# Projection, norm and turns chained per 128 tokens, layer parameters and sine tables loaded elsewhere

## The chip, the cores and the metric

One core of a Trainium2 chip runs the whole program; the metric is device time in microseconds (us) of one execution. TensorE (PE) multiplies and turns tiles, VectorE (DVE) and ScalarE (ACT) do the elementwise work, GpSimd (POOL) splits weights, and the queue of SyncE (SP) starts the weight DMAs.

## The reference

Four layers run over 512 tokens of width 1024, all in float32: two of a first kind (differential attention beside an mLSTM), two of a second kind (retention beside stick-breaking attention, then an MLP). What matters here is their frame:

```python
h = rmsnorm(x, g)            # x * rsqrt(mean(x*x) + eps) * g, per token
proj = h @ w_in              # then the branches, a gated merge u
x = x + u @ w_o              # the projection back
# second kind only:
h = rmsnorm(x, g_mlp); x = x + relu(h @ w_up)**2 @ w_down
# at the end
return rmsnorm(x, g_final)
```

The first kind also needs `cos` and `sin` of position times 32 frequencies. So there are seven norms: one of the input, five between a projection back and the next matrix product, and the last, whose result is the output.

## The kernel before

Every float32 operand of a large product is held as a rounded high part and a low remainder, and a product is three matmuls (low x high, high x low, high x high; `product`, lines 554 to 558). A weight panel is 128 x 1024. Panels pass through a ring of four slots: SP loads one (line 453) once the panel four before it is `used`, POOL makes `w_hi` (line 537) and `w_lo` (line 540) of it and raises `split`, and PE uses it. `gemm` (line 560) takes one panel as eight 128 x 128 weights against 512 tokens, 24 matmuls, into bank 0 or 1. `project` (line 576) takes tokens as the stationary side: for each panel, two 128-row tiles of it for each of the four blocks of 128 tokens, 24 matmuls too, into banks 2 to 5 (`xb`). It runs twice, for each half of the 1024 columns of `x`, over four panels (eight behind the MLP).

The turn from one layer part to the next runs in this order. When the last panel's matmuls of block b end, DVE adds bank b into `x` (line 1373). ACT sums the squares of the new half (line 1004), and takes the root of the mean by Ln and Exp (lines 990, 991). DVE, after its four adds and, where a layer loop ends there, after the jump back, scales `x` into `xn` (line 1356). PE turns `xn` by matmuls against the identity (line 605, `norm_turns`): sixteen of 128 x 128 for channel tiles 0 to 3, then four for each of the tiles 4 to 7, each as soon as its bank is free. For every tile ACT copies the bank times the gain column `g_norm` into `h_hi` (line 1013), and DVE makes `h_lo` (line 1359). The first `gemm` waits for the tiles one by one (`fresh`, line 568).

In a layer of the first kind ACT starts the four parameter loads (lines 1020 to 1026) at the head of the layer, after the first add of x, and DVE's `lambdas` (line 1377) runs behind the norm. At the start of the program DVE works out angles on 128 x 512 elements (lines 1675 to 1698), ACT takes their sines, and only then come the input's squares. SP starts the loads of `x` after the positions and constants are in (lines 470, 471).

Engines are ordered by semaphores alone, each in program order. The layers are loops: two turns of a body of the first kind, two of the second, so the norms behind the first layer of each kind stand right behind a jump back on DVE and PE.

## Time and profile before

| | us |
|---|---|
| median of 3 runs | 3386.95 |
| lowest and highest | 3380.55, 3393.57 |
| the profiled execution | 3382.91 |
| its span, first to last instruction | 3381.1 |

The profile is of one execution. A row of the timeline is a start, a duration, an engine, a line, an operation, output<-inputs and shapes; several like instructions in a row are merged with a count. PE is matmuls, PEld weight loads. A matmul's duration includes its passage through the array, so the step from one start to the next is its cost. In brackets stands the idle time of the engine before it, and what ended that.

### The profile page before, as it was taken

How to read it: one execution, taken by the hardware profiler on the slowest of the kernel's cores; microseconds unless marked ns; L12 is line 12 of the kernel's file. 1: busy time of each engine (PE TensorE's matmuls, PEld its weight loads, DVE VectorE, ACT ScalarE, POOL GpSimd, SP SyncE). 2: the span in 40 equal slices, each digit the busy share in tenths (PEclk: the TensorE clock that was granted, in tenths of full speed). 3: DMA queues.
4: the chain of work that ended last, by engine and by line, in shares of the span. 5: the costliest groups of instructions: out<-in, count | busy, mean ns of one | idle time of the engine just before them, and what ended most of it. 6: DMA issues, size and time to landing. Idle time of an engine off the chain costs nothing.

```text
span 3381.1 us, 47060 instructions
## 1 busy us (share of the span) xinstructions
PE 3251.9 (96%) x15456; PEld 2691.9 (80%) x15456; DVE 1437.8 (43%) x2325; ACT 820.0 (24%) x1773; POOL 1821.1 (54%) x1028
## 2 busy tenths in 40 slices
PE   5998999998998999999999999999899999999998
PEld 4877888886777888878887887888788888878887
DVE  7777462117776642126666112111166662121011
ACT  4554332014554331022222002101122220021020
POOL 3444455663444555655455665666554555656664
PEclk9999999999999999999999999999999999999999
DMA  3222222222221222232222222222222222222322
GB/s 106 75 89 67 69 75 81 98 98 63 87 87 57 76 73 89 98 102 84 75 84 78 90 96 88 94 99 95 83 84 84 75 83 87 99 87 94 99 93 99
DMA packets 87983, 290.54 MB, mean 86 GB/s; under 512 B 12833, under 2 KB 13537, under 8 KB 87921
## 3 DMA queue, kind: packets, MB, share of 16 engines
q1 hardware_dynamic: 75024, 273.12, 24.3%
q10 hardware_dynamic: 12896, 16.64, 1.8%
q8 instruction: 34, 0.56, 0.1%
q14 instruction: 29, 0.23, 0.0%
HBM read 275.00 MB, written 2.10 MB: 82 GB/s over the span
## 4 chain that ended last, share of the span: by engine, by line
PE 87%; DVE 7%; issue 3%; ACT 1%; ACTq 1%; DVEq 0%; DMA 0%
PE bank L556 27%; PE bank L558 27%; PE bank L557 27%; PE bank L624 1%; DVE xq L1416 1%; PE bank L742 1%; PE bank L605 1%; PE bank L653 1%; DVE k_hi L1347 1%; ACTq L1032 1%; PE bank L775 1%; DVE xk L1416 1%; DVE xn L1356 0%; DVE xk L1412 0%; PE bank L715 0%
## 5 line engine op out<-in xcount | busy, mean ns | idle before, releaser
L537 POOL TENSOR_SCALAR w_hi<-raw 128x1024 fp32r<-128x1024 f32 x512 | 560.6, 1095 | 1493.7 <-DMA raw<-in_w_in 1026.9
L540 POOL TENSOR_TENSOR w_lo<-raw,w_hi 128x1024 fp32r<-128x1024 f32 x512 | 1260.4, 2462 | 42.7
L556 PE MATMUL bank<-h_lo,w_hi 128*128 128x512 f32 x2816 | 1118.4, 397 | 0.6 <-DVE h_lo L1359 0.3
L558 PE MATMUL bank<-h_hi,w_hi 128*128 128x512 f32 x2816 | 1099.9, 391 | 0.0
L557 PE MATMUL bank<-h_hi,w_lo 128*128 128x512 f32 x2816 | 1098.7, 390 | 0.0
L558 PEld LDWEIGHTS bank<-h_hi,w_hi 128*128 128x128 f32 x2816 | 530.4, 188 | 113.2
L556 PEld LDWEIGHTS bank<-h_lo,w_hi 128*128 128x128 f32 x2816 | 531.4, 189 | 108.8 <-issue 2.5
L557 PEld LDWEIGHTS bank<-h_hi,w_lo 128*128 128x128 f32 x2816 | 531.6, 189 | 106.0
L1373 DVE TENSOR_TENSOR x<-x,bank 128x512 f32 x64 | 44.0, 688 | 458.1 <-PE bank L558 458.1
L556 PE MATMUL bank<-w_lo,up_hi 128*128 128x512 f32 x512 | 199.2, 389 | 0.0
L557 PE MATMUL bank<-w_hi,up_lo 128*128 128x512 f32 x512 | 199.2, 389 | 0.0
L558 PE MATMUL bank<-w_hi,up_hi 128*128 128x512 f32 x512 | 199.2, 389 | 0.0
L1553 DVE TENSOR_TENSOR sig_b<-bank,sig_b 128x512 f32<-128x512 f32 x32 | 22.1, 692 | 326.0 <-PE bank L558 326.0
L1347 DVE TENSOR_SCALAR up_hi<-mm 128x512 f32 x64 | 28.9, 451 | 272.1 <-ACT mm L1309 272.1
L1307 ACT ACTIVATE m<-bank 128x512 f32<-128x512 f32 x64 | 38.4, 601 | 437.7 <-PE bank L558 437.7
L1548 DVE TENSOR_TENSOR sig_a<-bank,sig_a 128x512 f32<-128x512 f32 x32 | 22.1, 692 | 230.1 <-PE bank L558 230.1
L556 PEld LDWEIGHTS bank<-w_lo,up_hi 128*128 128x128 f32 x512 | 96.1, 188 | 19.9
L557 PEld LDWEIGHTS bank<-w_hi,up_lo 128*128 128x128 f32 x512 | 96.1, 188 | 19.9
L558 PEld LDWEIGHTS bank<-w_hi,up_hi 128*128 128x128 f32 x512 | 96.1, 188 | 19.9
L556 PE MATMUL bank<-a_lo,w_hi 128*128 128x512 f32 x256 | 101.1, 395 | 4.2 <-DVE a_lo L1348 4.2
L557 PE MATMUL bank<-a_hi,w_lo 128*128 128x512 f32 x256 | 101.0, 395 | 0.0
L1080 ACT ACTIVATE sig_b<-bank 128x512 f32<-128x512 f32 x32 | 19.2, 600 | 336.9 <-PE bank L558 336.9
(297 smaller groups left out, 4520.1 us busy)
## 6 DMA issues: line engine op xcount, KB each, us to landing
raw<-in_w_in SPq DMA_DIRECT2D x288, 512.0 KB, 3.3
raw<-in_w_up SPq DMA_DIRECT2D x64, 512.0 KB, 3.3
raw<-in_w_down SPq DMA_DIRECT2D x64, 512.0 KB, 3.2
raw<-in_w_out_a SPq DMA_DIRECT2D x16, 512.0 KB, 3.2
raw<-in_w_out_b SPq DMA_DIRECT2D x16, 512.0 KB, 3.3
...
```

The costliest lines, as they stand in the source:

```text
L537: nc.gpsimd.tensor_scalar(m.w_hi[:, slot], m.raw[:, slot], 1.0, 0.0, ALU.mult, ALU.add).then_inc(s["w_step"], 1)
L540: nc.gpsimd.tensor_tensor(m.w_lo[:, slot], m.raw[:, slot], m.w_hi[:, slot].bitcast(F32), ALU.subtract).then_inc(s["split"], 1)
L556: nc.tensor.matmul(dst, hi, rhs_lo, start=first, stop=False, **more)
L557: nc.tensor.matmul(dst, lo, rhs_hi, start=False, stop=False, **more)
L558: return nc.tensor.matmul(dst, hi, rhs_hi, start=False, stop=last, **more)
L605: return nc.tensor.transpose(xb[k % TB][:, b * P:b * P + P], m.xn[:, b, k * P:k * P + P], m.ident[:])
L624: mm = nc.tensor.transpose(dst[:, b * P:b * P + P], src(b), m.ident[:])
L653: mm = nc.tensor.matmul(sq[k][qb], q[r, tok], key[r, keys], start=part == 0, stop=part == 2)
L1307: own(activation(m.m[j % 2][:], acc[c][:], ACT.Relu))
L1347: own(ts(hi, src, 1.0, None, ALU.mult))
L1373: tt(xs, xs, xb[b][:], ALU.add).then_inc(s["x_done"], 1)
L1416: ins = tt(x[:], x[:], rstd[0][:], ALU.mult)
```

## The change

- The product of the last half of every projection is done in another order: all panels but the last three as before, then, for each block of 128 tokens, its three held panels (`HELD`). The three panels are thus given back during the last block. In the other halves one panel is held, which changes nothing.
- PE turns block 0 between the blocks 1 and 2 of that half, block 1 between 2 and 3, and blocks 2 and 3 after it (`turn_block`), each as eight turns into two banks.
- DVE alternates: add of a block, `xn` of it (now with the gain, loaded as a row on all partitions, `g_row`, by `scalar_tensor_tensor`), `h_lo` of the block before. ACT alternates likewise. On DVE and ACT the norm now stands ahead of the jump back; on PE the turns of blocks 2 and 3 stand behind it.
- The first two panels behind a norm are done together in halves of 256 tokens (`first_panels`): panel 0 early tokens, turn of block 3, panel 1 early tokens, then both for the late tokens. The first attention turn of a second-kind layer and parts of the MLP are written out for that.
- The next layer's parameters are loaded, and `lambdas` computed, during the projection.
- At the start `x` is loaded without a wait, the angles are 128 x 128 (32 frequencies for four blocks), ACT writes their sines four times side by side, and PE turns them into the tables.
- Input and output norm use the same functions; PE and ACT turn and copy the last norm too, though only `xn` is used.

```diff
+        turned = [[m.bank[6], m.bank[2]], [misc, m.bank[3]], [m.bank[6], m.bank[4]], [m.bank[3], m.bank[5]]]
...
-            sp.wait_ge(s["pos_in"], 16)
-            sp.wait_ge(s["const_in"], 16 * 2)
...
+            def first_panels():
+                slots = [(at.n.get("panel", 0) + i) % RING for i in range(2)]
+                banks = [acc[(at.n.get("acc", 0) + i) % 2] for i in range(2)]
+                def half(i, tok):
+                    for k in range(KT):
+                        w = slice(k * P, k * P + P)
+                        mm = product(banks[i][:, tok], m.w_hi[:, slots[i], w], m.w_lo[:, slots[i], w],
+                                     m.h_hi[:, k, tok], m.h_lo[:, k, tok], k == 0, k == KT - 1)
+                    return mm
+                early, late = slice(0, 2 * P), slice(2 * P, S)
+                turn_block(2)
+                pe.wait_ge(s["split"], at.at("panel", 1))
+                pe.wait_ge(acc_free[at.n.get("acc", 0) % 2], at.at("acc", 2, div=2))
+                pe.wait_ge(s["h_ready"], at.at("norm", times=KT) + TB)
+                half(0, early)
+                turn_block(3)
+                pe.wait_ge(s["split"], at.at("panel", 2))
+                pe.wait_ge(acc_free[(at.n.get("acc", 0) + 1) % 2], at.at("acc", 3, div=2))
+                half(1, early)
+                pe.wait_ge(s["h_ready"], at.at("norm", times=KT) + KT)
+                at.add("norm")
+                for i in range(2):
+                    half(i, late).then_inc(s["used"], 1)
+                at.add("panel", 2)
+                at.add("acc", 2)
...
+            def project(x_hi, x_lo, tiles, ready, before, last):
+                count = tiles // 2
+                held = HELD if last else 1
+                def part(q, b):
+                    slot, tok = (at.n.get("panel", 0) + q) % RING, slice(b * P, b * P + P)
+                    for k in range(2):
+                        w = slice(k * 512, k * 512 + 512)
+                        kt = 2 * q + k
+                        mm = product(xb[b][:], x_hi[:, kt, tok], x_lo[:, kt, tok], m.w_hi[:, slot, w],
+                                     m.w_lo[:, slot, w], kt == 0, kt == tiles - 1)
+                    return mm
+                for q in range(count - held):
+                    pe.wait_ge(s["split"], at.at("panel", q + 1))
                     pe.wait_ge(s[ready], before + (2 * q + 2))
                     for b in range(TB):
-                        tok = slice(b * P, b * P + P)
                         if q == 0:
                             pe.wait_ge(s["x_done"], at.at("xb", times=TB) + (TB + b + 1))
-                        for k in range(2):
-                            w = slice(k * 512, k * 512 + 512)
-                            kt = 2 * q + k
-                            mm = product(xb[b][:], x_hi[:, kt, tok], x_lo[:, kt, tok], m.w_hi[:, slot, w],
-                                         m.w_lo[:, slot, w], kt == 0, kt == tiles - 1)
-                        if q == tiles // 2 - 1 and b < TB - 1:
-                            mm.then_inc(s["xb_done"], 1)
+                        mm = part(q, b)
                     mm.then_inc(s["used"], 1)
-                    at.add("panel")
+                for b in range(TB):
+                    for q in range(count - held, count):
+                        if b == 0:
+                            pe.wait_ge(s["split"], at.at("panel", q + 1))
+                            pe.wait_ge(s[ready], before + (2 * q + 2))
+                        mm = part(q, b)
+                        if b == TB - 1:
+                            mm.then_inc(s["used"], 1)
+                    if b < TB - 1:
+                        mm.then_inc(s["xb_done"], 1)
+                    if last and b in (1, 2):
+                        turn_block(b - 1)
...
+            def turn_block(b):
+                pe.wait_ge(s["xn_ready"], at.at("norm", times=TB) + (b + 1))
+                if b == 1:
+                    misc_bank()
+                elif b > 1:
+                    pe.wait_ge(s["h_ready"], at.at("norm", times=KT) + (1, 4)[b - 2])
+                for j in range(2):
                     for k in range(TB):
-                        mm = turn_block(k, b)
-                        if b == TB - 1:
-                            mm.then_inc(s["xT_done"], 1)
-                for k in range(TB, KT):
-                    pe.wait_ge(s["h_ready"], at.at("norm", times=KT) + (k - TB + 1))
-                    for b in range(TB):
-                        mm = turn_block(k, b)
+                        o = (j * TB + k) * P
+                        mm = nc.tensor.transpose(turned[b][j][:, k * P:k * P + P], m.xn[:, b, o:o + P], m.ident[:])
                     mm.then_inc(s["xT_done"], 1)
...
+            turn_block(0)
+            turn_block(1)
+            for k in range(2):
+                pe.wait_ge(s["trig_ready"], k + 1)
+                turn4(acc[k], lambda b: m.trig[:, k, b].rearrange("p r f -> p (r f)")).then_inc(s["trigT_done"], 1)
...
+            def h_high(b):
+                for j in range(2):
+                    act.wait_ge(s["xT_done"], at.at("norm", times=KT) + (2 * b + j + 1))
+                    activation(m.h_hi[:, j * TB:j * TB + TB, b * P:b * P + P],
+                               turned[b][j][:].rearrange("p (k t) -> p k t", t=P), ACT.Copy).then_inc(s["h_hi_ready"], 1)
...
+            def norm(gain):
+                act.wait_ge(s["x_done"], at.at("proj", times=KT) + 1)
+                act.dma_start(m.g_row[:], gain.to_broadcast([P, D])).then_inc(s["gain_in"], 16)
                 for b in range(TB):
                     act.wait_ge(s["x_done"], at.at("proj", times=KT) + (b + 1))
-                    ins = activation(m.junk[:, b], halves[:, b, 0], ACT.Square, accum_out=m.sm[:, b:b + 1])
-                own(ins)
-                own(activation(m.sm[:, 80:84], m.sm[:, 0:4], ACT.Identity, bias=m.col[:, 2:3], scale=1.0 / D))
+                    first_half_squares(b)
+                first_half_means()
                 for b in range(TB):
                     act.wait_ge(s["x_done"], at.at("proj", times=KT) + (TB + b + 1))
-                    own(activation(m.junk[:, b], halves[:, b, 1], ACT.Square, accum_out=m.sm[:, b:b + 1]))
-                    inv_sqrt(m.sm[:, 4 + b:5 + b], m.sm[:, b:b + 1], 1.0 / D, m.sm[:, 80 + b:81 + b], s["rms_ready"])
-            def norm(gain):
-                act.dma_start(m.g_norm[:], gain).then_inc(s["gain_in"], 16)
-                sums_of_squares()
-                act.wait_ge(s["gain_in"], at.at("norm", 1, times=16))
-                for k in range(KT):
-                    act.wait_ge(s["xT_done"], at.at("norm", times=KT) + (k + 1))
-                    activation(m.h_hi[:, k], xb[k % TB][:], ACT.Copy,
-                               scale=m.g_norm[:, k:k + 1]).then_inc(s["h_hi_ready"], 1)
+                    second_half_squares(b)
+                    root(b)
+                    if b:
+                        h_high(b - 1)
+                h_high(TB - 1)
+                at.add("norm")
...
+            def angles_out():
+                for k, angles in enumerate((m.red, m.red2)):
+                    act.wait_ge(s["angles_ready"], k + 1)
+                    activation(m.trig[:, k], angles[:].rearrange("p (b f) -> p b f", b=TB).unsqueeze(2)
+                               .to_broadcast([P, TB, 4, 32]), ACT.Sin).then_inc(s["trig_ready"], 1)
...
+            def norm_of_input():
+                squares_of_input(0)
+                squares_of_input(1)
+                angles_out()
+                log_exp_tables()
+                root(0)
+                root(1)
+                squares_of_input(2)
+                root(2)
+                h_high(0)
+                tables_out()
+                squares_of_input(3)
+                root(3)
+                for b in range(1, TB):
+                    h_high(b)
...
+                act.wait_ge(s["used"], at.at("panel", RING))
+                layer_parameters(l + 1)
+                skip_projection()
+                log_exp_tables()
+                lambda_exponents()
+                norm(t["gain_1"][bass.ds(l, 1)])
...
+            def normalised(b):
+                dve.wait_ge(s["rms_ready"], at.at("norm", times=TB) + (b + 1))
+                stt(m.xn[:, b], m.x[:, b], m.sm[:, 4 + b:5 + b], m.g_row[:], ALU.mult,
+                    ALU.mult).then_inc(s["xn_ready"], 1)
+            def h_low(b):
+                for j in range(2):
+                    dve.wait_ge(s["h_hi_ready"], at.at("norm", times=KT) + (2 * b + j + 1))
+                    tiles, tok = slice(j * TB, j * TB + TB), slice(b * P, b * P + P)
+                    ins = tt(m.h_lo[:, tiles, tok], turned[b][j][:].rearrange("p (k t) -> p k t", t=P),
...
+            def add_and_norm(tiles):
+                add_half(0, tiles)
+                at.add("panel", tiles // 2)
+                dve.wait_ge(s["gain_in"], at.at("norm", 1, times=16))
+                for b in range(TB):
+                    add_block(1, b)
+                    normalised(b)
+                    if b:
+                        h_low(b - 1)
+                h_low(TB - 1)
+                at.add("proj4")
...
-                add_to_x(KT)
+                lambdas()
+                add_and_norm(KT)
...
+            for b in range(TB):
+                ins = ts(m.ang[:, b * 32:b * 32 + 32], m.col[:, 8:40], m.posf[:, b:b + 1], None, ALU.mult)
+            own(ins)
```

On PE, at the end of a first-kind layer's last projection. `w_lo`, `u_hi` are parts of a panel and of the merged branches, `xn` the normalised tokens, `ident` the identity. Before:

```order
L557 MATMUL bank<-w_hi,u_lo 128x512
L558 MATMUL bank<-w_hi,u_hi 128x512
L136 REGISTER_ALU
L136 COMPARE_AND_BRANCH
L136 REGISTER_ALU
L136 COMPARE_AND_BRANCH
L136 UNCONDITIONAL_BRANCH
L136 ISA
L605 MATMUL bank<-ident,xn 128x128 x4
L610 REGISTER_ALU
```

Now, between the blocks 1 and 2 of the same projection:

```order
L561 MATMUL bank<-w_hi,u_lo 128x512
L562 MATMUL bank<-w_hi,u_hi 128x512
L650 REGISTER_ALU
L658 MATMUL bank<-ident,xn 128x128 x8
L560 MATMUL bank<-w_lo,u_hi 128x512
L561 MATMUL bank<-w_hi,u_lo 128x512
```

The turns of block 0, which all stood behind the projection, now stand within it; those of block 1 stand likewise one block later.

On DVE, at the same projection. `x<-x,bank` is the add, `sm` holds the root. Before:

```order
L1373 TENSOR_TENSOR x<-x,bank 128x512
L136 REGISTER_ALU
L136 COMPARE_AND_BRANCH
L136 REGISTER_ALU
L136 COMPARE_AND_BRANCH
L136 UNCONDITIONAL_BRANCH
L136 ISA
L1356 TENSOR_SCALAR xn<-x,sm 128x1024
L1355 REGISTER_ALU
L1356 TENSOR_SCALAR xn<-x,sm 128x1024
```

Now:

```order
L1470 TENSOR_TENSOR x<-x,bank 128x512
L1447 REGISTER_ALU
L1448 SCALAR_TENSOR_TENSOR xn<-x,sm,g_row 128x1024
L1453 REGISTER_ALU
L1455 TENSOR_TENSOR h_lo<-bank,h_hi 128x4x128
L1453 REGISTER_ALU
L1455 TENSOR_TENSOR h_lo<-bank,h_hi 128x4x128
L1466 REGISTER_ALU
L1470 TENSOR_TENSOR x<-x,bank 128x512
```

The add of a block, its `xn` and the `h_lo` of the block before follow each other, and no jump stands between the add and `xn`.

On PE, at the first panels of the second norm inside a second-kind layer. Before, the last turns led to a full panel:

```order
L617 REGISTER_ALU
L605 MATMUL bank<-ident,xn 128x128 x4
L136 UNCONDITIONAL_BRANCH x2
L136 ISA
L565 ISA
L556 MATMUL bank<-h_lo,w_hi 128x512
```

Now the turn of block 3 stands between half panels:

```order
L562 MATMUL bank<-h_hi,w_hi 128x256
L650 REGISTER_ALU
L658 MATMUL bank<-ident,xn 128x128 x8
L597 REGISTER_ALU
L560 MATMUL bank<-h_lo,w_hi 128x256
L561 MATMUL bank<-h_hi,w_lo 128x256
```

PE has the early tokens of panel 0 to do while block 3 is normalised.

## Rows read from the trace of the kernel before

**Rows 1.** The page: busy time and share of the span, by engine.

```profile
PE 3251.9 (96%) x15456; PEld 2691.9 (80%) x15456; DVE 1437.8 (43%) x2325; ACT 820.0 (24%) x1773; POOL 1821.1 (54%) x1028
```

**Rows 2.** What PE waited for: us in total, times, longest.

```profile
PE bank L605 <- DVE xn L1356: 51.6, 8, 29.2
```

**Rows 3.** Timeline of the third norm, behind the second layer: DVE, ACT, PE.

```profile
1493.61 0.69 DVE L1373 TENSOR_TENSOR x<-x,bank 128x512 f32 x1 [16.99 <-PE bank L558]
1494.33 0.63 ACT L1004 ACTIVATE junk<-x 128x512 f32<-128x512 f32 x1 [16.46 <-DVE x L1373]
...
1495.42 0.20 ACT L991 ACTIVATE sm<-sm 128x1 f32<-128x1 f32 x1
...
1498.30 3.45 DVE L1356 TENSOR_SCALAR xn<-x,sm 128x1024 f32<-128x1024 f32 x4
...
1499.81 3.49 PE L605 MATMUL bank<-ident,xn 128*128 128x128 f32 x16 [2.27 <-DVE xn L1356]
...
1502.70 4.88 ACT L1013 ACTIVATE h_hi<-bank,g_norm 128x512 fp32r<-128x512 f32 x8 [3.00 <-PE bank L605]
...
1503.42 5.36 DVE L1359 SCALAR_TENSOR_TENSOR h_lo<-bank,g_norm,h_hi 128x512 fp32r<-128x512 f32 x8 [1.67 <-ACT h_hi L1013]
...
1504.22 2.63 PE L605 MATMUL bank<-ident,xn 128*128 128x128 f32 x16 [0.93 <-DVE h_lo L1359]
```

**Rows 4.** Timeline of POOL at the same norm.

```profile
1495.71 1.06 POOL L537 TENSOR_SCALAR w_hi<-raw 128x1024 fp32r<-128x1024 f32 x1 [1.96 <-DMA raw<-in_w_in]
1496.85 2.36 POOL L540 TENSOR_TENSOR w_lo<-raw,w_hi 128x1024 fp32r<-128x1024 f32 x1
1501.24 1.41 POOL L537 TENSOR_SCALAR w_hi<-raw 128x1024 fp32r<-128x1024 f32 x1 [2.03 <-DMA raw<-in_w_in]
```

**Rows 5.** Timeline of PE: last projection products and first panel, third and fifth norm.

```profile
1496.93 0.39 PE L557 MATMUL bank<-w_hi,u_lo 128*128 128x512 f32 x1
1497.16 0.39 PE L558 MATMUL bank<-w_hi,u_hi 128*128 128x512 f32 x1
...
1506.74 0.47 PE L556 MATMUL bank<-h_lo,w_hi 128*128 128x512 f32 x1
...
2429.74 0.39 PE L558 MATMUL bank<-w_hi,up_hi 128*128 128x512 f32 x1
...
2445.26 0.47 PE L556 MATMUL bank<-h_lo,w_hi 128*128 128x512 f32 x1
```

**Rows 6.** Timeline of DVE at the fifth norm, across the jump back.

```profile
2430.27 0.69 DVE L1373 TENSOR_TENSOR x<-x,bank 128x512 f32 x1 [0.67 <-PE bank L558]
2434.94 1.17 DVE L1356 TENSOR_SCALAR xn<-x,sm 128x1024 f32<-128x1024 f32 x1 [3.98 <-issue]
```

**Rows 7.** DMA queues from 761 to 763 us, at the second norm: packets, MB, share.

```profile
q8 instruction: 1, 0.02, 3.9%
```

**Rows 8.** Timeline of PE: products of 256 columns in the retention's values.

```profile
1543.28 0.28 PE L556 MATMUL bank<-rv_lo,sw_hi 128*128 128x256 f32 x1
1543.40 0.28 PE L557 MATMUL bank<-rv_hi,sw_lo 128*128 128x256 f32 x1
```

**Rows 9.** Timeline of POOL and DVE: two operations over each other.

```profile
792.24 2.68 POOL L540 TENSOR_TENSOR w_lo<-raw,w_hi 128x1024 fp32r<-128x1024 f32 x1
...
792.73 2.73 DVE L1416 TENSOR_TENSOR xq<-xq,sq_q 128x512 f32<-128x512 f32 x1
```

**Rows 10.** Timeline of the start.

```profile
4.51 0.43 DVE L1675 CAST ang<-posi 128x512 f32<-128x512 int32 x1 [4.51 <-DMA col<-in_cst]
...
15.96 1.28 ACT L1184 ACT_TABLE_LOAD   x1 [15.96 <-DVE red L1696]
...
36.27 0.47 PE L556 MATMUL bank<-h_lo,w_hi 128*128 128x512 f32 x1
```

**Rows 11.** Timeline of the end.

```profile
3371.78 0.39 PE L558 MATMUL bank<-w_hi,up_hi 128*128 128x512 f32 x1
...
3372.91 4.87 DVE L1829 SCALAR_TENSOR_TENSOR xn<-x,sm,g_fin 128x1024 f32<-128x1024 f32 x4
```

269 lines of the change are left out of this document (141 added, 128 removed).

## The prediction

> **What bounds the kernel now.** PE does, nearly everywhere: it is busy 96% of the span and no other engine passes 54% [rows 1]. The change leaves the number of products as it is, so its gain can only come from the 4% in which PE stands. Of what PE waits for, the turns of the norm come first: 51.6 us for `xn`, 29.2 of them the start of the program [rows 2]. I read then one norm in the timeline [rows 3]. From 1493.61 on DVE adds, ACT squares and takes the root, but `xn` of block 0 begins only at 1498.30, when all four adds are done, though its root was there at 1495.62; sixteen turns end with block 3, ACT copies from 1502.70, and the other sixteen turns go at the pace of DVE. PE's last projection product starts at 1497.16, its first panel product at 1506.74: 9.58 us [rows 5]. The fourth and sixth norm read alike (9.50 and 9.41). The second and fifth, behind a jump back, take longer: 15.52 for the fifth [rows 5], 15.38 for the second. There DVE stands 3.98 us for nothing but its own instructions before `xn` [rows 6].
>
> **The stage after the change, from L, the start of the last projection product.** Steps: products of 512 columns are 0.227 apart [rows 5], of 256 columns 0.12 [rows 8], eight turns take 1.3 (sixteen in 2.63 [rows 3]), say 1.35 with the switch.
> Before: from L to the end of the second panel are 9.58 + 48 x 0.227 = 20.5 us, in the fifth norm 26.4.
> Inside the projection, two turns of a block are added: 2.7. Block 0's turn needs `xn` at 4.1 us (18 products) after the block's end. The add starts 0.5 behind the last product, the root is there 2.0 behind the add (1493.61 to 1495.62 [rows 3]), and `xn` with the gain row takes 4.87 / 4 = 1.22 to 1.28 [rows 11]: 3.9, just in time. But POOL begins the split of a panel 4.1 after its last use (1497.16 to 1501.24 [rows 4, 5]) and is at it for 1.1 + 2.4 (1495.71 to 1499.21 [rows 4]). The panel before the held ones is used 4.1 before the end of block 0, so its `w_lo` runs over the moment when `xn` 0 wants to start. DVE operations on two SBUF tiles do stand behind POOL's `w_lo`: 2.73 instead of 0.69 [rows 9]. That makes `xn` 0 about 0.9 late and PE wait 0.5. Insertion: 3.2.
> Behind L: turn 2 (1.35), 24 half products (2.9), turn 3 (1.35), 72 half products (8.65), and 0.2 to L's own end: 14.5 without waits. The 96 half products cost 11.5 where 48 full ones cost 10.9; that is in it.
> Two waits can stand in this. Turn 3 needs `xn` 3: root at L + 2.6, `xn` at L + 3.9, wanted at L + 4.5. The first held panel is free 2.7 before L, so POOL's first operation on its successor starts at L + 1.4 and `w_lo` runs from L + 2.5 to L + 4.9. `xn` 3 asks at L + 2.6: a tie. If `w_lo` has begun, `xn` ends at L + 6.2 and everything is 1.75 late. If `xn` is first, `w_lo` slips and panel 1 is split at L + 6.4, when PE wants it at L + 5.9: 0.5. In the second and fifth norm POOL began 4.8 after the last use (0.7 later than in the others), so `xn` slips in between POOL's two operations, and panel 1 comes 1.0 late.
> I take the blocked case, the order that the sum gives by 0.1 us. Third, fourth and sixth norm: 3.2 + 14.5 + 1.75 = 19.5 against 20.5, 20.4, 20.3: 1.0 + 0.9 + 0.8 = 2.8 us gained. Second and fifth: 3.2 + 14.5 + 1.0 = 18.7 against 26.3 and 26.4: 15.3 gained.
> The Trainium skill (SBUF — State Buffer, "SBUF: two separate sides") says that a DVE operation with two SBUF inputs and a GpSimd operation lock each other out for the whole instruction. By that rule the trace agrees for a `tensor_tensor` [rows 9]; no row shows the `scalar_tensor_tensor` under a long POOL operation. By this rule the blocked case stands.
>
> **Where DVE's jump goes.** It now comes behind the last `h_lo`, at L + 7.4 (L + 9 if blocked), and costs 4 [rows 6]: done by L + 11.4. DVE's next work is the squares of panel 0, ready at L + 12.5. ACT's jump comes at L + 6.6 and has the same cover. Both hide behind the 72 half products; without that cover they would cost up to 4 each. PE's own jump is now uncovered: turn 2 stands right behind it. Within 2 us of the second norm's L (760.61) 0.02 MB of instructions are fetched [rows 7], but before the change PE waited 6 us there anyway, so the price isn't visible. Bounds: 0 and DVE's 4.0 per jump; a gain is excluded, since the jump stays and nothing covers it any more. I take 0.75 for each of the two, because 1.0 of wait for panel 1 absorbs the first of it: -1.5.
> The Trainium skill (Runtime: NRT & Kernel Launch, "Instruction fetch mechanics") speaks against the change here: a taken branch whose target isn't in the window stalls until the page is fetched. By it the two jumps would cost PE what they cost DVE, 8 instead of 1.5.
>
> **The held panels and the loads.** The slot of the last held panel comes free at the end of the half before, and the panel is wanted 8.4 us later, as the third of block 0 (24 + 12 products of 0.227 and the switch); free to split is 4.1 + 3.5 = 7.6. Slack 0.8, from which a 512 KB gain row beside it takes up to 1: -0.7 over all. The parameter loads and `lambdas` move to a stretch in which DVE waits 17 us for the bank (1493.61 [rows 3]): nothing, and nothing was gained, since they lay beside PE's first panel. SP has no more instructions than before. On DVE's first-layer chain the two panels now end 2.9 apart instead of 5.4, POOL's splits fall more on the rotations: each hit is up to 2 us, in two layers; I take -1.0 (0 to -4).
>
> **The start.** First product at 36.27 now, end of panel 1 at 47.2 [rows 10]. After: constants at 4.5 [rows 10], four parameter issues, squares of blocks 0 and 1 (0.82 per half and 0.3 between, 2.1 each) to 11.9; 22 small operations on DVE end before that. Two sines, the table (1.28 [rows 10]), roots: 15.6. `xn` 0 and 1 under POOL's four splits: 18 to 21; turns, tables, squares of block 3, root, copy of block 1: 29 to 30; `h_lo` 31. Then 96 half products and turn 3, 12.9, and some switching: end of panel 1 at 44.7. Gain 2.5; with `xn` never blocked 5, with every block behind POOL 0.
>
> **The end.** Before 3381.1 - 3371.78 = 9.35 [rows 11], for `xn` of four blocks and the last store. After, `xn` 3 stands at L + 3.9 and the store 3.3 later, but the turns, copies and `h_lo` that nobody reads end at L + 7.6, and L is 3.2 later: 10.8. Loss 1.45.
>
> **Sum.** 2.8 + 15.3 - 1.5 - 0.7 - 1.0 + 2.5 - 1.45 = 16.0. Against the profiled execution's 3382.91 that is 3366.9; it ran 4.0 below the median, so for a median of runs 3386.95 - 16.0 = 3371.0.
>
> **Rivals.** *`xn` 3 goes first* in the three short norms: 1.25 more in each, and with panel 1 hidden in all five up to 5.7: 3371.0 - 3.8 = 3367. For it: the tie is 0.1 us. Against: the rows give POOL the lead.
> *PE's jump is hidden and the start is not blocked*: 1.5 + 2.5 more, with the former 3363. For it: fetches start before the engine gets there.
> *PE stalls at its jumps and the held panels come late.* By DVE's price the jumps cost 8 instead of 1.5. If three loads that are asked for 1.4 us apart land together, as late as the last one, the first comes 2.7 later, panel 1 at L + 7.6 in place of 4.9 and PE waits 2.5 more in five norms, 12.5. Together 19.0 more than the forecast: 3390, slower than before. It decides from 2.4 us per norm on, if both jumps stall. Against: the panel loads now land in 3.2 to 3.3 us each behind each other's tail, and only one is in flight at most times.
> *The change doesn't do what it says*: turns within the projection would wait for `xn`. From 2.5 us of wait at both turns in five norms the gain is gone: 3387, no change. POOL's 0.9 would have to be a whole `w_lo` and ACT's copy both times.
>
> **Chances.** Forecast (3371, itself 3366 to 3376) 0.48; `xn` first 0.22; hidden jump and quick start 0.12; no change 0.11; stalls 0.07. 0.5% is 16.9 us, about what a measurement of this kernel can tell from no change: below 3370.0 is faster. The forecast lies just above, so 0.18 of its 0.48 goes there, with nearly all of the next two, less what the runs' own spread takes: faster 0.46. Of the stalls the forecast of 3390 is itself within 0.5%; past 3404 it takes the worst of each term at once: slower 0.04, same 0.50. The range takes in the second and third and half of the fourth: 3358 to 3385.
>
> **What would show it.** Right: PE's wait for `xn` in five norms down to some us in all; last projection product to end of the second panel 16 in the short norms; no stop of DVE before `xn`, but one behind the last `h_lo`; `xn` of 1.3 us or 3 to 4 where POOL's `w_lo` is under way. Wrong: PE idle over 2 us between the last projection product and turn 2 (its jump), or before the early tokens of panel 1 (split); DVE's jump showing up as a wait of ACT or PE for the first squares; the first half product later than 32.

## The result and the profile after

The changed kernel takes 3366.24 us (median of 8 runs, 3357.35 to 3376.11) beside 3388.08 of the kernel before on the same chip (median of 8, 3380.55 to 3393.57): a ratio of 0.9937, 95% interval 0.992 to 0.9954, so 0.6% faster. The profiled execution took 3366.99, its span 3365.2; that of the kernel before 3382.91. The traces therefore have to explain 15.9 us; the medians stand 21.8 apart, and single runs of either kernel differ by over 10.

Busy time of the changed kernel, which answers to [rows 1]:

```profile
PE 3257.8 (97%) x15784; PEld 2713.4 (81%) x15784; DVE 1474.5 (44%) x2343; ACT 822.5 (24%) x1787; POOL 1827.3 (54%) x1028
```

PE is 6 us busier and waits 22 us less. L is again the start of the last projection product. The next view gives the stretch from L to the start of the last product of panel 1 for norms 2 to 6: its bounds, its length, busy us of PE, PEld, DVE, ACT and POOL, the granted clock, DMA share and GB/s. First the kernel before:

```profile
760.61:786.76 26.15, 17.48 (x81) 13.72 (x80) 14.68 (x26) 8.61 (x19) 6.91 (x5) 0.80 0.16 50
1497.16:1517.52 20.36, 17.16 (x82) 13.46 (x80) 9.43 (x14) 9.10 (x18) 6.32 (x4) 0.92 0.25 79
2072.20:2092.46 20.26, 16.39 (x82) 12.29 (x80) 10.71 (x15) 8.46 (x18) 7.35 (x5) 1.00 0.16 53
2429.74:2456.00 26.26, 17.66 (x82) 13.75 (x80) 10.26 (x14) 9.10 (x18) 6.36 (x4) 0.81 0.19 62
3014.31:3034.50 20.19, 16.41 (x82) 12.28 (x80) 10.62 (x15) 8.46 (x18) 7.03 (x5) 1.00 0.16 53
```

and the changed one:

```profile
767.62:782.91 15.29, 13.71 (x113) 13.21 (x112) 10.47 (x12) 4.47 (x10) 11.28 (x6) 1.00 0.34 111
1501.06:1518.03 16.97, 15.07 (x114) 14.77 (x112) 7.08 (x7) 5.16 (x10) 11.21 (x6) 0.90 0.45 147
2077.63:2092.28 14.65, 13.63 (x113) 13.29 (x112) 5.60 (x9) 4.62 (x10) 11.34 (x6) 1.00 0.35 117
2431.53:2446.19 14.66, 13.78 (x114) 13.35 (x113) 4.85 (x7) 5.16 (x10) 11.33 (x6) 1.00 0.40 133
3003.93:3019.39 15.46, 13.59 (x114) 13.29 (x113) 7.82 (x9) 4.60 (x10) 11.25 (x6) 1.00 0.34 112
```

Their sums are 113.2 and 77.0. From this 11.2 go for the turns that now stand inside the projections (2.0 to 2.4 each, in five), which leaves 25.0 us gained in the norms. Beside the length, read the clock: in the second and fifth norm PE had stood for 6.0 us before its first turn and for 1.6 more among the turns, and part of the stretch was at the lower of its two clock levels (1.2 GHz), a mean of 0.80 and 0.81; now the mean is 1.00.

What PE waits for now (total, times, longest), answering to [rows 2]:

```profile
PE bank L658 <- DVE xn L1448: 28.9, 10, 18.8
...
PE bank L692 <- DVE k_lo L1441: 7.2, 2, 3.7
PE bank L560 <- DVE rk_lo L1441: 5.6, 2, 2.9
PE bank L560 <- DVE h_lo L1455: 5.5, 1, 5.5
...
PE bank L560 <- DVEq L1740: 4.4, 2, 2.2
```

The wait for `xn` fell from 51.6 to 28.9, and 18.8 of that is the first turn of the program. The next three lines are where the gain went; the last comes up below. `k_lo` and `rk_lo` are the last steps of DVE's chain in the first head behind a norm of an attention-like layer (PE waited 1.7 in all for `k_lo` before, for `rk_lo` not at all); `h_lo` stands in the start.

The third norm in the timeline, answering to [rows 3, 4]: turn 2 right behind the projection (PE), the `xn` of block 3, POOL's `w_lo` of panel 1, and turn 3.

```profile
1501.30 1.03 PE L658 MATMUL bank<-ident,xn 128*128 128x128 f32 x8
...
1503.53 3.51 DVE L1448 SCALAR_TENSOR_TENSOR xn<-x,sm,g_row 128x1024 f32<-128x1024 f32 x1 [1.35 <-ACT sm L1037]
1503.58 2.38 POOL L544 TENSOR_TENSOR w_lo<-raw,w_hi 128x1024 fp32r<-128x1024 f32 x1
...
1507.10 1.11 PE L658 MATMUL bank<-ident,xn 128*128 128x128 f32 x8 [1.90 <-DVE xn L1448]
```

`xn` of block 3 takes 3.51 us instead of 1.28 and turn 3 waits 1.90. In the fourth norm the same two operations meet the other way round:

```profile
2080.10 1.28 DVE L1448 SCALAR_TENSOR_TENSOR xn<-x,sm,g_row 128x1024 f32<-128x1024 f32 x1 [1.35 <-ACT sm L1037]
2080.15 3.46 POOL L544 TENSOR_TENSOR w_lo<-raw,w_hi 128x1024 fp32r<-128x1024 f32 x1
```

`xn` was blocked in norms 2, 3 and 6 (3.32, 3.51, 3.49) and went first in 4 and 5. There it is panel 1 that comes late: PE waits 1.02 us for its `w_lo` in the fourth norm and 0.35 in the fifth.

The start, answering to [rows 10]: three `xn` on DVE, a `w_lo` of POOL, the sine table and the copy of blocks 1 to 3 on ACT, PE's first half product.

```profile
17.32 6.55 DVE L1448 SCALAR_TENSOR_TENSOR xn<-x,sm,g_row 128x1024 f32<-128x1024 f32 x3 [3.08 <-ACT sm L1037]
...
17.56 3.25 POOL L544 TENSOR_TENSOR w_lo<-raw,w_hi 128x1024 fp32r<-128x1024 f32 x1
...
25.67 0.69 ACT L1088 ACTIVATE sin<-bank,col 128x512 f32<-128x512 f32 x1 [4.34 <-PE bank L663]
...
29.52 2.04 ACT L1042 ACTIVATE h_hi<-bank 128x512 fp32r<-128x512 f32 x4
...
32.53 0.58 PE L560 MATMUL bank<-h_lo,w_hi 128*128 128x256 f32 x1 [5.47 <-DVE h_lo L1455]
```

Three `xn` take 6.55 us, the second of them 3.38. ACT then stands 4.34 us for the turns of the sines, which are queued on PE behind block 1's turns, and squares block 3 before it copies block 1 at 29.52. Panel 1 ends at 46.8, hardly ahead of the 47.05 before.

The end, answering to [rows 11]: last projection product and `xn` of block 3. The last `h_lo`, which nobody reads, ends 6.4 us behind the first of these lines.

```profile
3358.41 0.39 PE L562 MATMUL bank<-w_hi,up_hi 128*128 128x512 f32 x1
...
3360.88 1.29 DVE L1448 SCALAR_TENSOR_TENSOR xn<-x,sm,g_row 128x1024 f32<-128x1024 f32 x1 [1.35 <-ACT sm L1037]
```

From the last projection product to the end are 6.8 us, 9.35 before.

The ledger of the profiled executions, in us gained: norms with insertion 25.0; the first head behind the pair in four attention-like layers -17.25 (4.5, 3.5, 4.7, 4.6); start 0.3; end 0.8; and 7.1 in the long stretches between. Sum 15.9. Of the 7.1, 7.4 lie between the fifth and the sixth norm (2.0 between the third and the fourth, and 2.5 were lost in the layers of the first kind), and the change didn't aim at them. What the second kind gained there comes from another tie of DVE with POOL. In each retention head of a second-kind layer DVE splits the weighted scores into `sw_hi` and `sw_lo` and then makes `rv_lo`, for which PE waits (`DVEq L1740` in the list above; before the change it was `DVEq L1623`):

```profile
PE bank L556 <- DVEq L1623: 10.7, 5, 2.2
```

So five of the eight heads had this wait before and two have it now. One of the two, in the changed kernel:

```profile
1712.54 1.06 POOL L541 TENSOR_SCALAR w_hi<-raw 128x1024 fp32r<-128x1024 f32 x1 [2.56 <-DMA raw<-in_w_in]
1712.60 1.68 DVE L1440 TENSOR_SCALAR sw_hi<-om 128x1280 fp32r<-128x1280 f32 x1
...
1714.32 3.57 DVE L1441 TENSOR_TENSOR sw_lo<-om,sw_hi 128x1280 fp32r<-128x1280 f32 x1
...
1718.78 0.35 PE L560 MATMUL bank<-rv_lo,sw_hi 128*128 128x256 f32 x1 [2.22 <-DVEq L1740]
```

In the head before, `sw_hi` started at 1628.02, 0.19 ahead of `w_hi`; it took 0.83 and `sw_lo` 2.22, and PE didn't wait. In the traces of all kernels of this document the rule is the same: in the 52 heads in which `w_hi` started first, by 0.01 to 0.25 us, PE waited 1.96 to 2.26 us; in the 36 in which `sw_hi` started first or level with it, PE didn't wait (in 16 more, all of them first heads, no `w_hi` started near it). With the lower clock behind it such a wait costs up to 3.7 us (88.18 us from one `sw_hi` to the next in place of 84.53, in the kernel before). Nothing in the change was meant to decide this order, so this gain is luck as far as is known, and part of what single runs differ by may be the same; that isn't shown, as only one execution of each kernel was traced.

### The profile page after: what moved, and what is told of

Same layout as the page of the kernel before. It is cut to its first block, busy times and chain, and to the rows that moved or that the text cites. A ratio compares the mean times of both kernels' runs of the same rounds, so it can differ in the third digit from the quotient of the medians.

```text
span 3365.2 us, 47483 instructions
## 1 busy us (share of the span) xinstructions
PE 3257.8 (97%) x15784; PEld 2713.4 (81%) x15784; DVE 1474.5 (44%) x2343; ACT 822.5 (24%) x1787; POOL 1827.3 (54%) x1028
## 4 chain that ended last, share of the span: by engine, by line
PE 85%; DVE 9%; issue 3%; ACT 1%; ACTq 1%; DMA 1%; POOL 0%; DVEq 0%; SPq 0%; POOLq 0%
PE bank L560 27%; PE bank L562 26%; PE bank L561 26%; PE bank L663 1%; ACTq L1129 1%; DVE xq L1533 1%; PE bank L781 1%; PE bank L692 1%; DVE k_hi L1440 1%; DVE xn L1448 1%; DVE xk L1533 1%; PE bank L658 1%; PE bank L814 1%; DVE xk L1529 0%; DVE q_hi L1440 0%
## 5 line engine op out<-in xcount | busy, mean ns | idle before, releaser
L560 PE MATMUL bank<-h_lo,w_hi 128*128 128x512 f32 (+1 forms) x2912 | 1140.2, 392 | 7.0 <-DVE h_lo L1455 5.5
L562 PE MATMUL bank<-h_hi,w_hi 128*128 128x512 f32 (+1 forms) x2912 | 1119.8, 385 | 0.5 <-issue 0.5
L561 PE MATMUL bank<-h_hi,w_lo 128*128 128x512 f32 (+1 forms) x2912 | 1118.8, 384 | 0.0
L560 PEld LDWEIGHTS bank<-h_lo,w_hi 128*128 128x128 f32 x2912 | 553.0, 190 | 113.5 <-DVE h_lo L1455 5.7
L562 PEld LDWEIGHTS bank<-h_hi,w_hi 128*128 128x128 f32 x2912 | 551.5, 189 | 109.6
L561 PEld LDWEIGHTS bank<-h_hi,w_lo 128*128 128x128 f32 x2912 | 553.1, 190 | 103.1
L1470 DVE TENSOR_TENSOR x<-x,bank 128x512 f32<-128x512 f32 x64 | 44.0, 687 | 391.6 <-PE bank L562 391.3
L560 PE MATMUL bank<-w_lo,u_hi 128*128 128x512 f32 x256 | 100.3, 392 | 0.0
```

Of the source, the lines that this page charges most:

```text
L560: nc.tensor.matmul(dst, hi, rhs_lo, start=first, stop=False, **more)
L561: nc.tensor.matmul(dst, lo, rhs_hi, start=False, stop=False, **more)
L562: return nc.tensor.matmul(dst, hi, rhs_hi, start=False, stop=last, **more)
L1470: tt(xs, xs, xb[b][:], ALU.add).then_inc(s["x_done"], 1)
```

## The experiments

Questions: is it GpSimd that takes back 17 us in the first heads, or the later end of panel 0? What do the half products, the three held panels and the place of the jump bring by themselves? Where is PE's jump? Why did the start gain nothing?

### Whole products for the pair (full_pair)

```diff
                 turn_block(2)
...
-                half(0, early)
                 turn_block(3)
...
-                half(1, early)
                 pe.wait_ge(s["h_ready"], at.at("norm", times=KT) + KT)
                 at.add("norm")
-                for i in range(2):
-                    half(i, late).then_inc(s["used"], 1)
...
+                gemm(m.h_hi, m.h_lo)
+                gemm(m.h_hi, m.h_lo)
```

(Two waits ahead of each early half go too, and are done by `gemm`.)

> The first two panels of a stage in whole products (512 columns) behind turn 2 and turn 3, with one wait for all of h; everything else as in the changed kernel. Theory A: the half products save what PE would wait for block 3's xn, copy and h_lo, and they are also the cause of most of what the attention-like stages give back (4.3 to 4.7 us per first head behind the pair), because they finish panel 0 only 2.9 us ahead of panel 1 instead of 5.4, so DVE's chain of the first head ends that much later against PE. Then from L to the end of panel 1 every norm takes 4 to 5 us longer than in the changed kernel (some 17 to 19 instead of 11.8 to 15.3 plus), the two stages of the up projection lose all of it (9 us), the start 3 to 5, the four attention-like stages get 2.5 to 4.5 of it back: in all 13 to 21 us slower than the changed kernel, 3380 to 3387 us. Theory B: what is given back has nothing to do with how the pair is cut: then nothing comes back and the kernel is 25 to 30 us slower than the changed one, 3391 to 3396.

Measured: 3388.43 us (10 runs, 3380.51 to 3398.09), ratio to the kernel before 1.0007 (0.999 to 1.0023): 22 slower than the changed kernel. Without the half products nothing is left of the gain. Windows of the second and fifth norm:

```profile
763.42:785.95 22.53, 16.18 (x66) 13.04 (x65) 9.68 (x12) 4.57 (x10) 12.00 (x8) 0.77 0.30 92
...
2443.65:2462.66 19.01, 14.64 (x65) 11.81 (x64) 4.86 (x7) 5.16 (x10) 11.81 (x7) 0.91 0.37 123
```

The five are 27.9 us longer than in the changed kernel (22.5, 22.6, 21.9, 19.0, 18.8 against 15.3, 17.0, 14.7, 14.7, 15.5). The two lines differ by the same tie: in the first PE waits 4.76 us for `xn` 3, and the mean clock is 0.77; in the second 2.62, and the clock is 0.91. In exchange the give-back is gone: 24.26, 24.22, 24.60 and 24.60 us from panel 1 to the end of the panel that follows the scores, in the four attention-like layers, which are the values before to 0.1 (24.16, 24.21, 24.57, 24.57). Theory A, a little over the upper end of its times.

### GpSimd held back in the first head (pool_hold)

```diff
-            with at.loop((DEPTH * (PANELS_L1 + PANELS_L2)) // RING, panel=RING):
-                for _ in range(RING):
-                    split_panel()
+            with at.loop(DEPTH, panel=PANELS_L1, a=A_HEADS):
+                splits(4)
+                pool.wait_ge(s["qk_ready"], at.at("a", 1, times=2))
+                splits(4)
+                ...
+            with at.loop(DEPTH, panel=PANELS_L2, r=R_HEADS):
+                splits(5)
+                pool.wait_ge(s["rqk_ready"], at.at("r", 1, times=2))
+                splits(3)
+                ...
```

> Nothing is left out. GpSimd holds its next split of a panel back in the first head of every attention-like layer: in the first kind of layer all of panel 4 on until k_lo of the first head is written, in the second kind panel 5 on until rk_lo is. Theory A: the give-back behind the pair is DVE's chain of the first head being stretched by GpSimd's splits (2.8 us instead of 0.7 in 4 to 5 of its operations). Without them k_lo and rk_lo are written before PE asks: PE's waits of 7.2 us for k_lo and 5.6 us for rk_lo fall to under 1 each, 3 to 4 us gained in each of four stages: 11 to 15 us faster than the changed kernel, 3351 to 3355. Theory B: the chain is late because panel 0 ends later against panel 1, and its own length sets it: 0 to 3 us gained. Theory C: the held panels are then late themselves: PE waits for the split instead, no gain or a loss up to 5.

Measured: 3354.02 us (3344.7 to 3360.29), ratio 0.99 (0.9876 to 0.9924), 12 faster than the changed kernel. The waits for `k_lo` and `rk_lo` are gone from PE's list. The chain in the third stage, first in the changed kernel (two of DVE's ten steps, one of the four `w_lo` that POOL runs beside them, and the scores that wait):

```profile
1525.21 2.71 POOL L544 TENSOR_TENSOR w_lo<-raw,w_hi 128x1024 fp32r<-128x1024 f32 x1
1525.70 2.50 DVE L1440 TENSOR_SCALAR rq_hi<-rq 128x512 fp32r<-128x512 f32 x1
...
1535.18 2.70 DVE L1441 TENSOR_TENSOR rk_lo<-rk,rk_hi 128x512 fp32r<-128x512 f32 x1
...
1538.01 0.49 PE L560 MATMUL bank<-rq_lo,rk_hi 128*128 128x512 f32 x1 [2.86 <-DVE rk_lo L1441]
```

then with the hold:

```profile
1514.82 0.43 DVE L1455 TENSOR_SCALAR rk_hi<-rk 128x512 fp32r<-128x512 f32 x1
...
1516.20 1.05 POOL L541 TENSOR_SCALAR w_hi<-raw 128x1024 fp32r<-128x1024 f32 x1 [5.80 <-DVE rk_lo L1456]
```

From the first step to the end of `rk_lo` 17.5 us became 8.7; `rk_lo` itself takes 0.69. POOL stands 5.80 us for it. The stretch behind the pair, in the changed kernel:

```profile
1518.03:1547.26 29.23, 26.37 (x119) 21.98 (x118) 23.23 (x19) 3.48 (x6) 18.40 (x10) 0.94 0.30 95
```

and with the hold:

```profile
1504.27:1528.76 24.49, 24.49 (x118) 20.55 (x117) 15.13 (x18) 3.48 (x6) 15.99 (x10) 1.00 0.37 114
```

4.7 us less, of which 2.86 was the wait and most of the rest the lower clock behind it (0.94 against 1.00). All four stretches are back at the values before to 0.1 us (24.21, 24.16, 24.49, 24.50). Theory A; C fell.

The hold isn't free, though, and the list of PE's waits shows what it costs:

```profile
PE bank L575 <- DVEq L1755: 13.5, 7, 2.3
```

That is the wait for `rv_lo` of the section before, seven times in place of two. In the first head of a second-kind layer POOL now has panels to catch up with, `sw_hi` takes 2.21 and 2.00 us under its `w_lo` instead of 0.83, and PE waits 1.39 and 1.19; and in five of the six heads behind them `w_hi` is first. The long stretches took 11.2 us more than in the changed kernel, so that of the 17.4 us that the first heads won back the profiled executions show 6.7, and the medians 12.2. All four kernels with the hold have this wait in 7 or 8 of the eight heads, the nine without it in 1 to 5. How the hold shifts the order in the later heads wasn't looked into.

### The hold in the kernel before (before_hold)

The same edit, made to the kernel before, and nothing else.

> The kernel before, with the hold of GpSimd's splits in the first head of each attention-like layer and nothing else. Theory A: the give-back belongs to the half products, which leave DVE's chain 2.5 us less, so that GpSimd's splits decide; before, the chain had just the slack to absorb them (1.7 us of waiting for k_lo in two layers). Then the hold is worth 0 to 3 us here, 3385 to 3389 beside a kernel before of 3388. Theory B: the hold is an improvement by itself and only happens to stand beside the change: 8 to 14 us faster than before, 3375 to 3380.

Measured: 3388.21 us (10 runs), ratio 1.0009 (0.9997 to 1.0021). It is worth nothing there: theory A. The splits collided with the chain before as well [rows 9]; the chain had the slack for it, since panel 0 ended 5.4 us ahead of panel 1 and not 2.9. In the trace the hold takes away the one wait for `k_lo` (1.7 us) and 0.3 us of the first heads in all, and the waits for `rv_lo` are seven instead of five.

### Whole products and the hold (full_pair_hold)

The edits of full_pair and of pool_hold together.

> Whole products for the first two panels (as in the kernel with the whole pair, 3388) and GpSimd's hold in the first head of each attention-like layer (as in the kernel with the hold, 3354). Theory A: the give-back needs both, panel 0 finished late and GpSimd's splits on DVE's chain; whole products alone already take it away, so the hold has nothing left to win: 0 to 2 us faster than 3388, 3386 to 3388. The half products are then worth 22 us without the hold and 32 to 34 with it. Theory B: the two effects are independent and add up: 3388 - 12 = 3376.

Measured: 3395.47 us (8 runs, 3389.74 to 3403.49), ratio 1.0034 (1.002 to 1.0049). Neither theory: the effects don't add (B), but it is 7 us slower than whole products alone and not equal. The two profiled executions lie 20 us apart, further than the medians, and show two places. The windows of the fifth and sixth norm are 22.5 each in place of 19.0 and 18.8 (all five together 6.3 longer): in all five norms PE now stands 4.5 to 4.8 us before turn 3, so `xn` 3 lost every tie, and the clock is 0.77 in four of them. And the long stretches are 17.2 longer, with the wait for `rv_lo` in all eight heads instead of three. The first heads of the first kind gained 3.7 (22.40 each in place of 24.26 and 24.22). Whether the hold shifts the tie of `xn` 3 or the two profiles only fell differently isn't settled. What stands: the half products are worth 22 us without the hold and 41 with it.

### One panel held instead of three (held_one), and two (held_two)

```diff
-HELD = 3
+HELD = 1
```

(`HELD = 2` in the second.)

> Only the last panel of the second half is run block by block, instead of the last three; everything else as in the changed kernel, the turns of blocks 0 and 1 still stand inside the projection. Blocks now end 1.4 us apart instead of 4.1. Theory A: block 0's turns want xn 1.4 us after block 0's end, and it takes 3.9, and those of block 1 follow as closely, so PE waits 3.5 to 5.5 us in each of five norms: 18 to 27 us slower than the changed kernel, 3384 to 3393. Theory B: holding three panels is worth little, because DVE and POOL set the pace of the norm anyway: less than 8 us slower, below 3374.

> The last two panels of the second half are run block by block, in place of three (3366) or one (3404); everything else as in the changed kernel. Blocks end 2.7 us apart. Theory A: what counts is whether xn, which is there 3.9 us behind a block's end, or 4.6 where a w_lo stands in its way, comes before the turn that wants it. At two panels block 0's turn is wanted at 2.7, so PE waits 1.2 to 1.9, and block 1's the same, in each of five norms, while turn 2 and turn 3 behind the last product are as with three: insertion 4.6 to 6 us instead of 2.2, and 12 to 19 us slower than the changed kernel, 3378 to 3385, near the middle between one and three. Theory B: two panels already cover DVE, since xn of one block overlaps the next block's products: within 5 us of the changed kernel.

Measured: 3403.98 us with one (ratio 1.0058, 1.0039 to 1.0078) and 3396.57 with two (1.0034, 1.0016 to 1.0052), 38 and 30 slower than with three. The first theory in both, and both sizes too small. Block 0's turn inside the third projection, and turn 2, with one panel held (block 1's turn waits 2.04):

```profile
1505.55 1.09 PE L658 MATMUL bank<-ident,xn 128*128 128x128 f32 x8 [2.06 <-DVE xn L1448]
...
1514.52 1.75 PE L658 MATMUL bank<-ident,xn 128*128 128x128 f32 x7 [0.86 <-DVE xn L1448]
```

The last 48 products of a projection, with the turns among them, take 17.2 to 18.2 us with one held, 13.6 to 17.3 with two, 12.9 to 13.3 with three (10.88 before): inside the projection block 0's turn waits 2.1 with one held, 2.6 to 2.9 with two in four of the five norms, and at most 0.4 with three. What I had left out is what comes behind: DVE's queue now has `xn` and `h_lo` of the earlier blocks in front of block 3's add, so with two held `xn` 3 begins 4.1 behind L instead of 2.5 in four of the five norms, and turn 3 at 7.4 to 7.6 instead of 4.0 to 6.0.

### The place of the jump alone (jump_alone)

```diff
-                norm()
                 lambdas()
...
                 add_to_x(KT)
+                norm()
```

(DVE; the same on PE and ACT, in both kinds of layer, with one norm ahead of the first loop.)

> The kernel before with its norm unchanged, only put at the end of a layer, so ahead of the jump back instead of behind it; at the very end a set of turns and copies that nobody reads is added (10 us of the time or so, so the total says nothing). Theory A: the second and fifth norm then take what the others take, 20.3 to 20.6 us from the last projection product to the end of the second panel instead of 26.2 to 26.3: 11.7 of the gain of the changed kernel is the place of the jump alone, and the chaining has the rest. Theory B: the jump's price moves to PE or to the first squares of the head: the two windows stay over 22, or the scores of the second layer's first head come as late as before.

Measured: 3393.24 us in the one run, the added end included. Theory A fell: the second and fifth windows are 27.2 and 25.7 (26.2, 26.3 before), the others 21.2, 20.9 and 21.1 (20.4, 20.3, 20.2). DVE's stop is gone, but PE's is there, between its last turns and its first panel product (`issue` means that the engine waited for nothing that the profile shows):

```profile
774.24 0.94 PE L605 MATMUL bank<-ident,xn 128*128 128x128 f32 x5
778.84 0.79 PE L556 MATMUL bank<-h_lo,w_hi 128*128 128x512 f32 x1 [3.66 <-issue]
```

So PE's jump costs 3.7 us where it is exposed, nearly what DVE's does [rows 6], and putting the jump elsewhere gains nothing by itself.

### PE drained before its jump (pe_drained)

```diff
+            def drained():
+                pe.wait_ge(s["used"], at.at("panel", RING))
+                pe.sem_inc(s["pe_step"], 1)
...
                 project_merged()
+                drained()
```

(and the same line at the end of the body of a second-kind layer.)

> The changed kernel with one wait more: PE lets its last projection product finish before it jumps back to the head of a layer. Theory A: a jump of PE costs it 3.5 to 4 us, as it did between the last turn and the first panel product in the kernel with only the place of the jump changed (3.7 us of waiting for issue, twice); in the changed kernel it is hidden because PE's sequencer runs ahead of the array over the last products, none of which waits for anything, and takes the jump while they are still executed. Then turn 2 begins 3 to 4 us behind L in the second and fifth norm instead of 0.2, and their windows grow by 3 to 4 us each; the third norm, which follows without a jump but behind the same wait, grows by under 0.5. Theory B: the jump is free because its target was fetched long before: nothing moves by more than 0.5.

Measured: 3379.42 us in the one run. Last projection product and turn 2 at the second norm:

```profile
765.77 0.39 PE L562 MATMUL bank<-w_hi,u_hi 128*128 128x512 f32 x1
770.91 1.97 PE L658 MATMUL bank<-ident,xn 128*128 128x128 f32 x8 [4.75 <-issue]
```

Turn 2 begins 5.14 and 5.56 us behind L in the second and fifth norm, 1.10 in the third, which has the same wait and no jump; in the changed kernel it was 0.30 and 0.23. So the jump costs 4.0 to 4.5 us when PE comes to it with nothing queued, and nothing when it has products left to execute. The two windows grew by 5.4 and 5.5, more than expected, since the clock fell as well (0.84 and 0.92 against 1.00). Theory A. That the sequencer runs ahead of the array is the explanation that fits; the trace shows only when products start.

### `w_lo` behind `xn` of block 3 (xn_hold)

```diff
                 pool.wait_ge(s["w_step"], at.at("panel", 1, times=2))
+                if behind_xn:
+                    at.add("norm")
+                    pool.wait_ge(s["xn_ready"], at.at("norm", times=TB))
                 nc.gpsimd.tensor_tensor(m.w_lo[:, slot], ...
```

(`behind_xn` is set for the second panel behind each norm.)

> The changed kernel with one wait more: of every stage's second panel GpSimd writes w_hi as before, but starts w_lo only when xn of block 3 is written. Theory A: xn of block 3 and this w_lo exclude each other, and the one that is second pays for the other: in the changed kernel xn took 3.3 to 3.5 us in three norms and w_lo 3.5 in the other two. With the wait xn of block 3 takes 1.3 us in all five norms and in the start, the w_lo behind it 2.4, PE waits at turn 3 for nothing or a few tenths, and L to the end of panel 1 is 14.4 to 15.0 us in every norm (15.3, 17.0, 14.7, 14.7, 15.5 in the changed kernel): 3 to 4 us less in all. Theory B: they don't lock each other out and xn 3 waits for something else in DVE's queue: xn stays at 3.3 us or more in some norms, and the windows grow by the later w_lo, 1 us each.

Measured: 3366.93 us in the one run. Third norm:

```profile
1500.04 1.28 DVE L1473 SCALAR_TENSOR_TENSOR xn<-x,sm,g_row 128x1024 f32<-128x1024 f32 x1 [1.35 <-ACT sm L1062]
...
1501.40 2.36 POOL L547 TENSOR_TENSOR w_lo<-raw,w_hi 128x1024 fp32r<-128x1024 f32 x1 [1.39 <-POOLq L540]
```

`xn` 3 takes 1.28 in all five norms, the windows are 14.87, 14.87, 14.89, 15.60 and 14.87, 1.9 us less in all: theory A, with half its size, since where `xn` had gone first the window is now 0.2 to 0.9 longer. Four of the five are equal to 0.02, so the tie was what made them differ; the fifth norm has a stop of its own (last section). In the 14.87 PE waits 1.25 for the later `w_lo`: the wait has moved from `xn` to the panel and become shorter. In the start, where the same wait keeps POOL from its second `w_lo` until `xn` 3, `xn` 0 to 2 take 1.28 each and panel 1 ends at 44.3 instead of 46.8. The total doesn't show the 1.9 and 2.5 us: they are less than runs of one kernel differ by, and in this trace one head more waits for `rv_lo` (three, in place of two).

### ACT's order in the start (start_order)

```diff
                 h_high(0)
-                tables_out()
                 squares_of_input(3)
                 root(3)
-                for b in range(1, TB):
+                h_high(1)
+                tables_out()
+                for b in range(2, TB):
                     h_high(b)
```

> The changed kernel with only ACT's order in the start altered: the squares of block 3 and the copy of block 1 ahead of the sine tables; GpSimd isn't held. Theory A: the two causes of the slow start overlap. The hold alone (in the kernel whose w_lo waits for xn) brought the end of panel 1 from 46.8 to 44.3, hold and order together to 37.8. With the order alone xn of block 1 still ends at 21.8, its turns at 23.7, the copy of block 1 at 25, DVE's h_lo of it at 26 to 27, and the tables at 26.5: first half product at 27 to 28.5 instead of 32.5, end of panel 1 at 40 to 42. Theory B: the first product waits for GpSimd's blocking of xn 1 to 3 in any case: 44 or later.

Measured: 3371.22 us in the one run; first half product at 28.71, end of panel 1 at 42.57. Theory A, half a microsecond late: the order alone is worth 4.2 us, the hold alone 2.5.

### Both holds and the order (both_holds)

> The changed kernel with both holds of GpSimd (the first head's, and w_lo of the second panel behind xn of block 3) and one change of order in the start: ACT squares block 3 and copies block 1 before it writes the sine tables, instead of the tables, the squares of block 3, then the copy of block 1. Nothing is left out. The start: in the changed kernel the first half product began at 32.5, since xn of block 1 stood behind a w_lo until 21.8, ACT waited for the turns of the sines until 25.7 and came to the copy of block 1 at 29.5. With neither, xn 0 to 3 end by 24, the copy of block 1 is done by 24 and the tables by 26: first half product at 27 to 28.5, end of panel 1 at 42 to 43.5 instead of 46.8. Theory A: the three causes add up: 3354 of the first hold alone, less 3 to 5 for the start, less 3 to 4 for the norms: 3345 to 3348. Theory B: what is gained in the start is lost again in the first head, where the chain of DVE waits for the second parameter load, the masks and the lambdas behind the norm: 3350 to 3354.

Measured: 3348.92 us (3346.86 to 3354.07), ratio 0.9887 (0.9871 to 0.9904): 17 us under the changed kernel and 1.1% under the one before. It lies between the times of the two theories; against the hold alone (0.99) the intervals overlap, and the 5 us between the two medians are not more than likely. All of the computation is there. Its start, as above:

```profile
16.29 4.46 DVE L1476 SCALAR_TENSOR_TENSOR xn<-x,sm,g_row 128x1024 f32<-128x1024 f32 x3 [3.21 <-ACT sm L1064]
...
25.47 0.39 PE L587 MATMUL bank<-h_lo,w_hi 128*128 128x256 f32 x1 [1.16 <-DVE h_lo L1483]
```

Panel 1 ends at 37.83, 9.0 earlier than in the changed kernel, where 2.5 and 4.2 add up to 6.7. Of the rest 1.0 is an earlier first `xn` (16.29 in place of 17.32), for which the edit gives no reason, and the remainder goes with the clock: 1.00 over this start, 0.96 with the order alone, 0.92 with the hold alone and 0.93 in the changed kernel, whose first half products run 0.21 apart instead of 0.12. The profiled executions add up: 6.7 of the hold, 9.0 and 1.9 make 17.6, and 18.6 was measured. Here too PE waits for `rv_lo` in seven heads, 11.7 us in all, so some of what the holds gain is lost again there.

## Why the prediction was right, and where it was not

The forecast was 3371.0 in a range of 3358 to 3385; 3366.2 was measured. The sign and the size came out, and the profiled gain is the 15.9 that the sum gives. But the terms are not those of the sum: the norms were 8.4 better than predicted, the first heads 16.25 worse, and 7.1 came from stretches that had no term. That they cancel is luck. The medians, 21.8 apart, are 5.8 further apart than the forecast had them.

| term (us gained) | predicted | in the traces |
|---|---|---|
| norms 3, 4, 6 | 2.8 | 6.8 |
| norms 2, 5, with PE's jumps | 15.3 - 1.5 | 18.2 |
| held panels | -0.7 | none seen |
| first heads | -1.0 | -17.25 |
| start | 2.5 | 0.3 |
| end | -1.45 | 0.8 |
| rest | 0 | 7.1 |

- **The norms** were under-sized. "Insertion: 3.2" measured 2.0 to 2.4. `xn` 0 was blocked as foreseen (2.10 and 2.15 us in the second and third norm, in place of 1.28), and PE waited at most 0.4 for it; but eight turns cost 0.80 to 0.85 us until the next product begins, not 1.35. The price was half of sixteen turns in 2.63 [rows 3], and those went at the pace of DVE, as the text says of them itself. The same two turns make "from L on 14.5 without waits" too long: less its waits the stretch is 13.6 to 13.8 us where the clock held. The tie fell both ways. Blocked, PE waited 1.6 to 1.9 us, near the 1.75 of the sum; with `xn` first it waited about 1.0, for panel 1, where the text had 0.5. Between the two orders lie 0.6 and 0.8 us where the clock held, 2.3 where it didn't. POOL wasn't later in the second and fifth norm: its `w_lo` began 2.3 and 2.5 us behind L, and 2.5 in the others. What the lower clock had cost in these two norms stood unnamed in the sum, as part of the measured 26.3 and 26.4. And the gain rests on all parts together: without the half products 22 us are gone, with two panels held in place of three 30.
- **"Where DVE's jump goes"** was right, it is hidden: in the second norm DVE stops 2.36 us for issue behind its last `h_lo`, and PE doesn't wait. **PE's jump** at 0.75 each was too dear by all of it, and the reason in the text (a wait for panel 1 absorbs it) was the wrong one. The products queued before it cover it; uncovered it would have been 4.0 to 4.5, at or over the upper bound given. Only the stop of 0.53 in the fifth norm (last section) may belong to it.
- **The first heads** are the term that failed most: "POOL's splits fall more on the rotations: each hit is up to 2 us, in two layers; I take -1.0 (0 to -4)". The mechanism was the right one, named with the 2.9 against 5.4 us that decides it, but the term left out the second kind of layer, put half a microsecond per layer where four steps of the chain take 2.5 to 2.9 and three more 1.3 to 1.4, and left out the clock behind the wait. It measured 17.25, and the hold shows that with POOL kept out of the chain nothing of it is left.
- **The start**: the blocked `xn` was foreseen at 18 to 21, the order on ACT was read ("tables, squares of block 3, root, copy of block 1: 29 to 30", measured 29.5), and `h_lo` at 31. The first half product came at 32.5, later than the 32 that the prediction had named as a sign of being wrong; then the clock took some 2 more, which no term had.
- **The long stretches** had no term. Their 7.1 is what the tie of `sw_hi` with `w_hi` gave (9.6, with two waits in place of five), less 2.5 in the layers of the first kind, whose cause wasn't looked for.
- **The end** counted the insertion at 3.2 and 7.6 behind L for the unread copies; it was 1.7 and 6.8.
- **The rivals**: *`xn` 3 goes first* happened in two norms of five (the fourth, and the fifth, for which it wasn't meant); *PE's jump is hidden* came true, its quick start didn't; *stalls* and *doesn't do what it says* fell.

The tie was called one, and it is one. The Trainium skill (SBUF — State Buffer, "SBUF: two separate sides") has it that whichever starts first holds the ports for its whole instruction. The runs bear out the lock for `scalar_tensor_tensor` (3.51 against 1.28, and 1.28 every time once POOL is held), and starts in the records tell who holds it, down to 0.05 us. In the changed kernel and the five that keep its order there, `xn` 3 took 3.2 to 3.5 wherever `w_lo` started ahead of it or less than 0.05 behind, and 1.28 wherever it was 0.07 or more ahead. At 0.05 the records show both: 3.51 in the third norm, 1.28 in the fourth.

The Trainium skill (Runtime: NRT & Kernel Launch, "Instruction fetch mechanics") has a taken branch whose target isn't in the window stall until its page is there. Drained, PE shows that stall, 4.0 to 4.5 us; in the changed kernel, with products queued ahead, it doesn't appear before turn 2.
